# Turning activations into scan inputs: 32 transposes of 128x128 in place of 128 narrow ones

## The chip, the cores and the metric

The kernel runs on one core of one Trainium2 chip. The metric is the device time of one execution in microseconds, as the median of several runs. The profile is that of one further execution, whose span runs from its first to its last instruction.

## The reference, cut to what matters

Two blocks follow each other on a sequence of 256 rows of 2048 features. The first is a differential attention layer, a forgetting attention layer and their layer norms. The second is an S5 layer (a diagonal state space model), a gated output and an MLP. The change lies in the S5 layer, in how its inputs `u` are laid out:

```python
def s5_mixer(h_ctx, h_lat, ...):
    u_ctx, u_lat = to_groups(h_ctx), to_groups(h_lat)     # (1, 256, 128 groups, 16 features)
    for direction in range(2):
        ...
        st_ctx = s5_scan(uc_ctx, lam_bar, b_bar, s0, reverse)
        s_ctx_final = st_ctx[:, 0] if reverse else st_ctx[:, -1]
        st_lat = s5_scan(uc_lat, lam_bar, b_bar, s_ctx_final, reverse)
        y_lat = y_lat + jnp.einsum('btgp,ghp->btgh', st_lat, c_mat).real
```

`h_ctx` and `h_lat` are RMS-normed rows, scaled and shifted per feature: `h = modulate(rmsnorm(x), shift, scale)`. The context comes from the inputs alone; the latent rows are the output of the first block.

## The kernel before

The 256 rows are handled as 32 chunks of 8 rows. The scan works on a tile `U` (for the context) or `UL` (for the latent rows) with 128 partitions and 4096 columns: a partition is one of the 8 rows of a chunk (`q`) with one of the 16 features of a group (`h`), and the columns are 128 groups by 32 chunks. All of this happens twice: **run 0** is for the context, early, in the middle of the projection of the first layer; **run 1** is for the latent rows, after the last layer norm of the first block.

For each run the rows lie in `HC` with partition (a, c), where `a` (0 to 3) is a quarter of the features and `c` (0 to 31) the chunk, and with 8 by 512 columns. Within a quarter the 32 groups are split as e (0, 1) and j (0 to 15). The steps are:

1. `u_norm` works out the factor of each row. `turn` (VectorE for even q, ScalarE for odd q) multiplies the rows by it and writes them to `HT[run]` with columns ordered e, j, q, h. So for one (e, j) the 128 columns (q, h) are contiguous, and the partitions are (a, c).
2. `u_turn` (TensorE, line 2545) turns these blocks. There are 8 pieces. Piece pc takes a = pc // 2 and e = pc % 2, and does 16 transposes, each of the 32 partitions of one a by 128 columns. Each gives 128 partitions by 32 columns of a bank of PSUM, and 16 fill the bank's 512 columns. The instruction is a load of 32x128 weights and a matmul that streams 32 columns of the identity matrix. In the trace all of them carry line 2553.
3. `u_piece` (VectorE, line 1904) empties a bank in two operations on 128x512 elements: a multiplication by the scale of each group and feature (`FU[run]`, columns 0 to 127, one for each group, repeated over the 32 chunks) from PSUM to `U`, and, once that has ended, an addition of the shift (`FU[run]`, columns 128 to 255) in place. The helper `tt` at line 1424 records both, under the name `arena` in run 0 and `LT` in run 1.

The pieces use two banks of PSUM in turn (5 and 6), so that piece pc + 2 can be written once the first operation of piece pc has ended.

**Around run 0.** The projection streams its weights as 192 tiles of 128x512. ScalarE rounds a tile (line 972), VectorE subtracts for the rest (`tiles`, line 1424, `ring_lo`), TensorE does 6 matmuls for it (`pre_tile`, line 2279). The order is written out by hand: `U_AFTER = 180` puts one piece of `u_turn` behind each of the tiles 180 to 187, and VectorE runs two tiles ahead of the piece that it empties (`tiles(min(U_AFTER + pc + 2, ...))`, then `u_piece`). Behind the 192nd tile ScalarE copies the result, rounds the weights of the gate projection, and VectorE makes them ready; then come the 32 steps of `bl` (VectorE builds a 128x1024 matrix, TensorE turns it by 8 transposes of 128x128, line 2282; the matrices are stored as `m_state`; `v_chunk` multiplies them with `U`).

**Around run 1.** The layer norm ends, the rows are copied by DMA into `HC`, are scaled, and then TensorE does all 8 pieces in a row. Its next instruction, `v_chunk` for `("vl", f, i)`, waits for all of `u_made`. That stage is 1024 small matmuls (line 2279, `bank<-LT,ring`), in two halves f of 512; the scan of half f on VectorE (31 steps of four operations of 128x128 on `state(f, k)`, one after the other) needs the half's results, and the output matmuls of half f need the last step of its scan.

SyncE issues the loads of all weights in a fixed order to 6 slots (`ring`, line 701); each load waits until the slot's last reader is done.

Of the kernel before, what the change touches and what calls it, by code (L numbers as in the profile page):

```python
# [11 lines left out]
MUL, ADD, SUB, MAX, MIN = ALU.mult, ALU.add, ALU.subtract, ALU.max, ALU.min  # L12
# [269 lines left out]
def build(nc, A, out):  # L282
    ctx = ExitStack()
    with ctx:
# [18 lines left out]
        def filled(*key):  # L303
            i, n = bank_t.at[key]
            return FILLED[i], n

        def emptied(*key):
            i, n = bank_t.at[key]
            return EMPTIED[i], n

        def fill(*key):
            return FILLED[bank_t.at[key][0]], 1

        def bank(*key):
            return banks[bank_t.at[key][0]]
# [11 lines left out]
        ident = sb("ident", 128)  # L327
# [37 lines left out]
        def reg(off, n):  # L365
            return AR[:, off:off + n]
# [127 lines left out]
        def bl_at(b):  # L494
            return *bls[b % 2], bt
# [11 lines left out]
        HT = [reg(off, 4096).rearrange("p (e g q h) -> p e g q h", e=2, g=16, q=8) for off in (R3, 24576)]  # L507
        u_of, FU, FU_made = (U, UL), (reg(R5 + 3712, 256), LT[:, 4096:4352]), L1[:, 2048:2304]
# [33 lines left out]
        def a_p(i):  # L542
            return wk[i % 4].rearrange("p (c s) -> p c s", c=2)[:, :, 0:128 * (i % 2 + 1)]

        def a_stat(i):
            return stat[:, 8 * (i % 6):8 * (i % 6) + 8]
# [4 lines left out]
        def a_av(i):  # L551
            return aT_[:, i % 3 * 2:i % 3 * 2 + 2, :].rearrange("p a b -> p (a b)")
# [20 lines left out]
        def toep_at(i):  # L573

            return i // 4 + i % 4 // 2 * 2
# [844 lines left out]
        def vector_program(v):  # L1420
            o = Order(S)

            def tt(dst, x, y, op, *to):
                return v.tensor_tensor(dst, x, y, op).then_inc(*(to or o.up("dve")))  # L1424
# [16 lines left out]
            def empty(*key):  # L1441
                o.own = emptied(*key)
                return o.own[0], 1

            def own():
                v.wait_ge(*o.own)
# [451 lines left out]
            tiles(KK_AFTER[15] + 1)  # L1898
            corners(15)

            def by_group(run, i, n):
                return FU[run][:, i * 128:i * 128 + 128].unsqueeze(2).to_broadcast([128, 128, 32])[:, n, :]

            def u_piece(run, pc):

                gs = slice(16 * pc, 16 * pc + 16)
                v.wait_ge(*filled("u", run, pc))
                y = u_of[run][:, gs, :]
                tt(y, bank("u", run, pc)[:, :].rearrange("p (g c) -> p g c", g=16), by_group(run, 0, gs), MUL, *empty("u", run, pc))
                own()  # L1910
                tt(y, y, by_group(run, 1, gs), ADD, *o.up("u_made"))

            def u_norm(run):
                v.wait_ge(*filled("ss", run))
# [60 lines left out]
            for pc in range(8):  # L1975
                tiles(min(U_AFTER + pc + 2, 16 * N_PRE))
                u_piece(0, pc)
# [35 lines left out]
            for t in range(21):  # L2013
                if 0 <= t - 3 < 16:

                    i = t - 3
                    p, s_ = a_p(i), a_stat(i)
# [7 lines left out]
                if 0 <= t - 4 < 16:  # L2025
                    i = t - 4
# [9 lines left out]
                if 0 <= t - 1 < 16:  # L2036
                    i = t - 1
                    h, t2 = i // 2, i % 2
                    w_ = 128 * (t2 + 1)
                    p, s_ = a_p(i), a_stat(i)  # L2040
# [52 lines left out]
            for n in range(N_W1):  # L2093
# [35 lines left out]
                elif n == N_K + 5:  # L2129
# [3 lines left out]
                    for g3 in range(3):  # L2133
                        copy(lf3[:, :, 32 * g3:32 * g3 + 16], lf)
                        at = slice(32 * g3, 32 * g3 + 16)
# [33 lines left out]
            for pc in range(8):  # L2169
                u_piece(1, pc)  # L2170
# [106 lines left out]
        def tensor_program(p):  # L2277
            def mm(dst, l_, r_, start, stop):
                return p.matmul(dst, l_, r_, start=start, stop=stop, skip_group_check=True)  # L2279

            def tr(dst, src, k=128):
                return p.transpose(dst, src, ident[0:k, 0:k])  # L2282
# [3 lines left out]
            def room(*key):  # L2286

                i = bank_t.at[key][0]
                if i in said:
                    p.wait_ge(*emptied(*said[i]))  # L2290
                said[i] = key
# [212 lines left out]
            for j in range(8):  # L2504
# [4 lines left out]
                if j == 4:  # L2509
                    p.wait_ge(S["lam_cols"], 1)  # L2510
                    room("lam")
                    for i, s_ in enumerate((cr, ci, lbr, lbi)):
                        t = tr(bank("lam")[:, 128 * i:128 * i + 128], s_)
# [29 lines left out]
                t.then_inc(*fill("kk", ch))  # L2543

            def u_turn(run, pc):
                a_, e = pc // 2, pc % 2
                at = slice(32 * a_, 32 * a_ + 32)
                if pc == 0:
                    p.wait_ge(S["turn_v"], 4 * (run + 1))
                    p.wait_ge(S["turn_a"], 4 * (run + 1))  # L2550
                room("u", run, pc)
                for j in range(16):
                    t = p.transpose(bank("u", run, pc)[:, 32 * j:32 * j + 32], HT[run][at, e, j, :, :].rearrange("p q h -> p (q h)"),  # L2553
                                    ident[at, at])
                t.then_inc(*fill("u", run, pc))

            def u_sums(run):
# [22 lines left out]
            for pn in range(N_PRE):  # L2580
                for k in range(16):
                    pre_tile(16 * pn + k)
                    if pn == 1 and k < 8:
                        state(2 * k)
                        state(2 * k + 1)
                    for ch in range(16):
                        if KK_AFTER[ch] == 16 * pn + k + 1:
                            corners(ch)
                    done = 16 * pn + k + 1
                    if done == FU_AFTER:  # L2590
                        unit_factors()
                    if done == SS_AFTER:
                        u_sums(0)
                    if 0 <= done - U_AFTER < 8:
                        u_turn(0, done - U_AFTER)
                if pn in MOD_AT_PRE:
                    mod(MOD_AT_PRE[pn])
                if pn in SUMS_AT_PRE:
                    sums(SUMS_AT_PRE[pn])
# [13 lines left out]
            for b in range(33):  # L2613
                if b < 32:
                    p.wait_ge(S["blm"], b + 1)
                    for r in range(2):
                        room("bl", b, r)
                        for j in range(4):
                            t = tr(bank("bl", b, r)[:, 128 * j:128 * j + 128], bl_at(b)[r][:, 128 * j:128 * j + 128])
# [8 lines left out]
                if b in PART_AT_BL:  # L2628
                    j, q = PART_AT_BL[b]
# [6 lines left out]
            for t_ in range(21):  # L2636
                if 0 <= t_ - 5 < 16:
                    i = t_ - 5
                    h, t2 = i // 2, i % 2
# [4 lines left out]
                    for s in range(t2 + 1):  # L2644
                        t = mm(bank("ao", i)[:, 0:256], a_av(i)[:, 128 * s:128 * s + 128], vN[0][:, s, 256 * h:256 * h + 256],
                               s == 0, s == t2)
                    t.then_inc(*fill("ao", i))
                if 0 <= t_ - 4 < 16:
                    i = t_ - 4
                    p.wait_ge(S["amix"], i + 1)  # L2650
                    room("at", i)
                    for s in range(i % 2 + 1):
                        t = tr(bank("at", i)[:, 128 * s:128 * s + 128], wk[i % 4][:, 128 * s:128 * s + 128])
                    t.then_inc(*fill("at", i))
                if t_ < 16:
                    h, t2 = t_ // 2, t_ % 2
                    w_ = 128 * (t2 + 1)
                    room("as", t_)
                    for c in range(2):
                        t = mm(bank("as", t_)[:, 256 * c:256 * c + w_], qT[0][:, 2 * h + c, 128 * t2:128 * t2 + 128],  # L2660
                               kT[0][:, 2 * h + c, 0:w_], True, True)
                    t.then_inc(*fill("as", t_))
                if t_ in PART_AT_A:
                    j, q = PART_AT_A[t_]
# [6 lines left out]
            for n in range(N_W1):  # L2671
# [13 lines left out]
                if n == N_K + 6:  # L2685
                    room("nFT")
                    p.wait_ge(S["lf3"], 1)
                    for s in range(2):
                        t = mm(bank("nFT")[0:96, 0:256], lf3[:, s, :], tri[:, s, :], s == 0, s == 1)
                    t.then_inc(*fill("nFT"))  # L2690
                    room("FN")
                    for t2 in range(2):
                        for s in range(t2 + 1):
                            t = mm(bank("FN")[:, 16 * t2:16 * t2 + 16], tri[:, s, 128 * t2:128 * t2 + 128], lf[:, s, :], s == 0, s == t2)
# [9 lines left out]
            for pc in range(8):  # L2704
                u_turn(1, pc)
# [6 lines left out]
            for f in range(2):  # L2712
                p.wait_ge(S["step"], 31 * (f + 1))
                for i in range(4):
# [4 lines left out]
                    for i2 in (i, i + 4):  # L2719
                        cl[i2] = slot("cl", f, i2).rearrange("p (b d r x) -> p b d r x", b=2, d=4, r=2)  # L2720
                        e = toep_at(i2 - g4)
# [5 lines left out]
                    for j in range(4):  # L2727
# [7 lines left out]
                        for n, (i2, g2) in enumerate(four):  # L2735
                            t = mm(out_[n], UL[:, 32 * f + 4 * i2 + j + 64 * g2, :], wt[i2][:, 2 * (4 * g4 + j) + g2, :], False, True)
# [3 lines left out]
                for k in range(4 * f, 4 * f + 4):  # L2740
                    room("z", k)
                    for q in range(4):
                        t = tr(bank("z", k)[:, 128 * q:128 * q + 128], Y[:, k // 2, 4 * (k % 2) + q, :, :].rearrange("p g h -> p (g h)"))
# [63 lines left out]
```

## Time and profile before

| | |
|---|---|
| median of 3 runs | 2623.46 us (2622.78 to 2623.96) |
| span of the profiled execution | 2622.4 us |
| TensorE busy | 2418.2 us (92%) |
| VectorE busy | 1792.9 us (68%) |
| ScalarE busy | 1052.0 us (40%) |
| transposes of run 0 and run 1, line 2553 | 256, busy 22.0 us |

The time of the profiled execution by itself is not given, only its span; the median of the runs lies 1.1 us above that span. Busy time of TensorE counts each matmul until its result is out, so that overlapping ones make it look full; what a group of matmuls costs is read from the starts of its first instruction and of the first one behind it. `PEld` is the load of weights, which overlaps `PE`. A granted clock of 1.00 is 2.4 GHz and one of 0.50 is 1.2 GHz.

### The profile page before, as it was taken

What the parts mean: (1) busy time and instruction counts of PE and PEld (TensorE: products, weight loads), DVE (VectorE), ACT (ScalarE), POOL (GpSimd) and SP (SyncE); (2) the same over time, 40 slices, a digit from 0 to 9 for tenths busy, and PEclk for the clock granted to TensorE, in tenths of its full rate; (3) what the DMA queues carried; (4) which work ended last, traced back from release to release, by engine and by line L of the source; (5) the groups of instructions that cost most, each with busy time, mean ns of one, the idle gap of its engine ahead of it and who ended that gap; (6) DMA issues with size and microseconds to landing.
All of it is one profiled execution on the core that took longest, in us unless ns stands there. A gap on an engine that the chain in (4) does not pass through costs nothing.

```text
span 2622.4 us, 42441 instructions
## 1 busy us (share of the span) xinstructions
PE 2418.2 (92%) x17791; PEld 2018.3 (77%) x17791; DVE 1792.9 (68%) x2871; ACT 1052.0 (40%) x1588; POOL 183.4 (7%) x290
## 2 busy tenths in 40 slices
PE   5799999999889899989999696899799999999998
PEld 1488887777656698789887495688698998998986
DVE  4548887888767666877887648677654677655545
ACT  0243334454542323343662222444444443443443
POOL 1102433010100000112000000000000000000000
PEclk7699999999899899989999757999899999999999
DMA  9969999698877689979778897688455678655553
GB/s 352 338 233 345 364 363 323 205 344 321 302 292 274 225 305 327 379 267 316 241 256 312 230 338 298 221 283 278 140 181 189 225 272 281 216 184 189 190 166 108
DMA packets 317518, 699.75 MB, mean 267 GB/s; under 512 B 13648, under 2 KB 14160, under 8 KB 312464
## 3 DMA queue, kind: packets, MB, share of 16 engines
q1 hardware_dynamic: 298496, 627.29, 69.3%
q0 software_dynamic: 18560, 67.66, 7.2%
q8 instruction: 141, 2.31, 0.3%
q10 hardware_dynamic: 272, 2.10, 0.2%
q14 instruction: 49, 0.40, 0.0%
HBM read 646.78 MB, written 56.49 MB: 268 GB/s over the span
## 4 chain that ended last, share of the span: by engine, by line
PE 72%; DVE 13%; DMA 10%; ACT 2%; issue 1%; SPq 0%; DVEq 0%; POOL 0%; ACTq 0%
PE bank L2279 70%; DVE ring_lo L1424 3%; DMA ring<-in_w_mod 3%; DVE arena L1424 2%; DVE sm L1424 2%; DMA ring<-in_kv_w 2%; PE bank L2282 2%; DMA ring<-in_a_w_in 2%; DVE LT L1432 1%; DVE arena L1432 1%; DMA ring<-in_b_w_out 1%; PE bank L2553 1%; DMA m_state<-MSB 1%; DMA ring<-in_b_w_in 1%; ACT att_w_hi L1022 1%
## 5 line engine op out<-in xcount | busy, mean ns | idle before, releaser
L1424 DVE TENSOR_TENSOR ring_lo<-ring,w_hi 128x1024 fp32r<-128x1024 f32 (+1 forms) x380 | 428.2, 1134 | 355.0 <-ACT w_hi L1022 333.2
L1022 ACT CAST w_hi<-ring 128x1024 fp32r<-128x1024 f32 x316 | 330.2, 1048 | 471.8 <-PE bank L2279 471.7
L1022 ACT CAST att_w_hi<-ring 128x1024 fp32r<-128x1024 f32 x192 | 197.1, 1048 | 333.1 <-DMA ring<-in_kv_w 121.8
L1424 DVE TENSOR_TENSOR ring_lo<-ring,att_w_hi 128x1024 fp32r<-128x1024 f32 x192 | 233.8, 1221 | 132.0 <-ACT att_w_hi L1022 130.7
L2279 PE MATMUL bank<-in_hi,w_hi 128*128 128x256 f32 x1024 | 288.8, 282 | 1.1 <-ACT n L969 1.1
L2279 PE MATMUL bank<-in_lo,w_hi 128*128 128x256 f32 x1024 | 288.9, 282 | 0.0
L2279 PE MATMUL bank<-in_hi,ring_lo 128*128 128x256 f32 x1024 | 288.5, 282 | 0.0
L2279 PE MATMUL bank<-w_hi,hid_lo 128*128 128x512 f32 x640 | 254.2, 397 | 1.1 <-DVE ring_lo L1424 1.1
L2279 PE MATMUL bank<-att_w_hi,att_hi 128*128 128x512 f32 x512 | 211.6, 413 | 18.2 <-DVE ring_lo L1424 18.2
L2279 PE MATMUL bank<-ring_lo,att_hi 128*128 128x512 f32 x512 | 205.6, 402 | 0.0
L2279 PE MATMUL bank<-att_w_hi,att_lo 128*128 128x512 f32 x512 | 204.8, 400 | 0.0
L2279 PE MATMUL bank<-w_hi,hid_hi 128*128 128x512 f32 x512 | 202.6, 396 | 0.0
L972 ACT CAST in_lo<-ring 128x512 fp32r<-128x512 f32 x192 | 115.2, 622 | 215.2 <-PE bank L2279 117.7
L2279 PE MATMUL bank<-ring_lo,hid_hi 128*128 128x512 f32 x512 | 201.5, 394 | 0.0
L2279 PEld LDWEIGHTS bank<-in_hi,w_hi 128*128 128x128 f32 x1024 | 193.9, 189 | 1.4 <-ACT n L969 1.3
L2279 PEld LDWEIGHTS bank<-in_hi,ring_lo 128*128 128x128 f32 x1024 | 193.6, 189 | 0.0
L2279 PEld LDWEIGHTS bank<-in_lo,w_hi 128*128 128x128 f32 x1024 | 193.0, 188 | 0.1
L2279 PE MATMUL bank<-ring,cpad 128*32 128x512 f32 x1120 | 158.6, 674 | 22.6 <-DMA ring<-in_w_mod 18.3
L2279 PE MATMUL bank<-hid_lo,in_lo 128*128 128x256 f32 (+1 forms) x528 | 156.3, 296 | 15.6 <-DVE ring_lo L1424 15.2
L1424 DVE TENSOR_TENSOR ring_lo<-ring,in_lo 128x512 fp32r<-128x512 f32 x192 | 130.2, 700 | 55.8 <-ACT in_lo L972 55.7
L972 ACT COPY arena<-bank 128x512 f32<-128x512 f32 (+2 forms) x178 | 88.3, 582 | 172.7 <-PE bank L2279 154.7
L1432 DVE SCALAR_TENSOR_TENSOR LT<-ring,cpad,LT 128x512 f32<-128x512 f32 x195 | 146.7, 752 | 9.6
(278 smaller groups left out, 5106.1 us busy)
## 6 DMA issues: line engine op xcount, KB each, us to landing
ring<-in_w_mod SPq DMA_DIRECT2D x192, 1024.0 KB, 9.3
ring<-in_a_w_in SPq DMA_DIRECT2D x64, 1024.0 KB, 9.1
ring<-in_w_mlp_in SPq DMA_DIRECT2D x64, 1024.0 KB, 5.3
ring<-in_w_mlp_out SPq DMA_DIRECT2D x64, 1024.0 KB, 5.1
ring<-in_kv_w_mod SPq DMA_DIRECT2D x32, 1024.0 KB, 10.0
ring<-in_kv_w SPq DMA_DIRECT2D x32, 1024.0 KB, 7.9
ring<-in_b_w_in SPq DMA_DIRECT2D x32, 1024.0 KB, 5.7
ring<-in_s_w_glu SPq DMA_DIRECT2D x32, 1024.0 KB, 5.4
```

The source lines that it names most:

```text
L972: return a.copy(dst, src).then_inc(*(to or o.up("act")))
L1022: a.copy(whi(h), raw_half(h)).then_inc(*o.up("whi"))
L1424: return v.tensor_tensor(dst, x, y, op).then_inc(*(to or o.up("dve")))
L1432: return v.scalar_tensor_tensor(out=dst, in0=x, scalar=s1, in1=y, op0=o1, op1=o2).then_inc(*(to or o.up("dve")))
L2279: return p.matmul(dst, l_, r_, start=start, stop=stop, skip_group_check=True)
L2282: return p.transpose(dst, src, ident[0:k, 0:k])
L2553: t = p.transpose(bank("u", run, pc)[:, 32 * j:32 * j + 32], HT[run][at, e, j, :, :].rearrange("p q h -> p (q h)"), ident[at, at])
```

## The change

A piece now takes all four quarters a at once: pc gives e = pc // 4 and four values of j, and `u_turn` does 4 transposes of 128 partitions by 128 columns in place of 16 of 32 by 128. A bank then holds the columns (j, a, c). `u_piece` reads the bank in order, and the places in `U` and the factors in `FU` with strides: 4 values of j by 4 of a by 32 chunks, in runs of 32 columns, where before a piece was 512 contiguous columns of `U`. The number of elements, of pieces, of VectorE's operations, the banks and all waits are as before.

```diff
-            def by_group(run, i, n):
-                return FU[run][:, i * 128:i * 128 + 128].unsqueeze(2).to_broadcast([128, 128, 32])[:, n, :]
+            def by_group(run, i, e, j):
+                return (FU[run][:, i * 128:i * 128 + 128].rearrange("p (a e j) -> p e j a", a=4, e=2)[:, e, j]
+                        .unsqueeze(3).to_broadcast([128, 4, 4, 32]))
 
             def u_piece(run, pc):
 
-                gs = slice(16 * pc, 16 * pc + 16)
+                e, j = pc // 4, slice(pc % 4 * 4, pc % 4 * 4 + 4)
                 v.wait_ge(*filled("u", run, pc))
-                y = u_of[run][:, gs, :]
-                tt(y, bank("u", run, pc)[:, :].rearrange("p (g c) -> p g c", g=16), by_group(run, 0, gs), MUL, *empty("u", run, pc))
-                own()
-                tt(y, y, by_group(run, 1, gs), ADD, *o.up("u_made"))
+                y = u_of[run].rearrange("p (a e j) c -> p e j a c", a=4, e=2)[:, e, j]
+                tt(y, bank("u", run, pc)[:, :].rearrange("p (j a c) -> p j a c", j=4, a=4), by_group(run, 0, e, j), MUL,
+                   *empty("u", run, pc))
+                own()
+                tt(y, y, by_group(run, 1, e, j), ADD, *o.up("u_made"))
...
             def u_turn(run, pc):
-                a_, e = pc // 2, pc % 2
-                at = slice(32 * a_, 32 * a_ + 32)
+                e, j0 = pc // 4, pc % 4 * 4
                 if pc == 0:
                     p.wait_ge(S["turn_v"], 4 * (run + 1))
                     p.wait_ge(S["turn_a"], 4 * (run + 1))
                 room("u", run, pc)
-                for j in range(16):
-                    t = p.transpose(bank("u", run, pc)[:, 32 * j:32 * j + 32], HT[run][at, e, j, :, :].rearrange("p q h -> p (q h)"),
-                                    ident[at, at])
+                for j in range(4):
+                    t = tr(bank("u", run, pc)[:, 128 * j:128 * j + 128], HT[run][:, e, j0 + j, :, :].rearrange("p q h -> p (q h)"))
                 t.then_inc(*fill("u", run, pc))
```

## Rows read from the trace of the kernel before

**Rows 1.** Head of the page: span, TensorE's busy time.
```profile
span 2622.4 us, 42441 instructions
PE 2418.2 (92%) x17791; PEld 2018.3 (77%) x17791; DVE 1792.9 (68%) x2871; ACT 1052.0 (40%) x1588; POOL 183.4 (7%) x290
```

**Rows 2.** Timeline, run 0, one period: start us, length us, engine, operation, idle before.
```profile
467.00 1.07 PEld L2553 LDWEIGHTS bank<-ident,arena 32*128 32x128 f32 x16 [0.36 <-issue]
...
468.11 0.19 PEld L2279 LDWEIGHTS bank<-in_lo,hid_lo 128*128 128x128 f32 x1
...
468.22 0.69 DVE L1424 TENSOR_TENSOR arena<-bank,arena 128x512 f32<-128x512 f32 x1 [0.67 <-PE bank L2553]
...
468.94 0.69 DVE L1424 TENSOR_TENSOR arena<-arena 128x512 f32<-128x512 f32 x1
...
469.55 0.69 DVE L1424 TENSOR_TENSOR ring_lo<-ring,in_lo 128x512 fp32r<-128x512 f32 x1
469.70 1.07 PEld L2553 LDWEIGHTS bank<-ident,arena 32*128 32x128 f32 x16 [0.36 <-issue]
```

**Rows 3.** Chain that ended last, end of run 0: start us, length us, what.
```profile
484.33 7.20 PE bank L2279 x30
...
492.04 0.63 ACT w_hi L972
```

**Rows 4.** Windows, run 0: us, busy of PE, PEclk, DMA share, GB/s.
```profile
470.00:475.00 5.00, 5.00 (x43) 1.00 0.02 5
```

**Rows 5.** Timeline: transposes of 128x128 at clock 1.00 and at 0.50.
```profile
505.65 0.85 PEld L2282 LDWEIGHTS bank<-ident,arena 128*128 128x128 f32 x8 [0.84 <-issue]
506.47 0.19 PEld L2279 LDWEIGHTS bank<-w_hi,hid_lo 128*128 128x128 f32 x1
...
1124.35 3.67 PE L2282 MATMUL bank<-ident,arena 128*128 128x128 f32 x16 [6.27 <-DVE arena L1429]
1125.50 1.02 ACT L969 ACTIVATE arena<-bank,MODC,st 128x256 f32<-128x256 f32 x2 [1.18 <-PE bank L2282]
```

**Rows 6.** Timeline: VectorE and TensorE behind run 0.
```profile
490.02 1.29 DVE L1424 TENSOR_TENSOR arena<-arena 128x512 f32<-128x512 f32 x2
...
491.37 0.86 PEld L2282 LDWEIGHTS bank<-ident,arena 128*128 128x128 f32 x8 [0.29 <-DVE arena L1424]
...
492.69 1.90 DVE L1424 TENSOR_TENSOR ring_lo<-ring,w_hi 128x512 fp32r<-128x512 f32 x3 [1.38 <-ACT w_hi L972]
```

**Rows 7.** Timeline, run 1: the turns and VectorE's pieces.
```profile
1509.78 12.52 PEld L2553 LDWEIGHTS bank<-ident,arena 32*128 32x128 f32 x128 [11.64 <-issue]
...
1511.73 0.69 DVE L1424 TENSOR_TENSOR LT<-bank,LT 128x512 f32<-128x512 f32 x1 [3.12 <-PE bank L2553]
...
1513.44 0.69 DVE L1424 TENSOR_TENSOR LT<-bank,LT 128x512 f32<-128x512 f32 x1 [0.29 <-PE bank L2553]
1514.16 0.69 DVE L1424 TENSOR_TENSOR LT<-LT 128x512 f32<-128x512 f32 x1
1514.77 0.68 DVE L1424 TENSOR_TENSOR LT<-bank,LT 128x512 f32<-128x512 f32 x1
...
1523.95 36.27 PE L2279 MATMUL bank<-LT,ring 128*64 128x32 f32 x676 [1.51 <-DVE LT L1424]
```

**Rows 8.** Windows, run 1 and the stage behind: us, busy of PE, PEclk, DMA share, GB/s.
```profile
1509.70:1522.50 12.80, 12.63 (x128) 0.50 1.02 426
...
1524.00:1560.00 36.00, 36.00 (x676) 0.50 0.91 315
```

**Rows 9.** Chain that ended last, from run 1 on.
```profile
1523.95 27.55 PE bank L2279 x512
...
1625.35 15.76 PE bank L2279 x379
```

**Rows 10.** Timeline: a VectorE operation that reads `state(f, k)` in four runs of 32.
```profile
1553.26 0.29 DVE L1424 TENSOR_TENSOR sm<-arena,LS 128x128 f32<-128x128 f32 x1
```

**Rows 11.** Chain that ended last, in the second layer.
```profile
1038.37 11.46 DMA ring<-in_kv_w
```

**Rows 12.** SyncE's waits over the span: us in total, times, longest us.
```profile
SPq L701 <- PE bank L2279: 1706.2, 396, 24.9
```

**Rows 13.** Timeline: 32 matmuls of the same form as behind run 1, at clock 1.00.
```profile
510.86 1.12 PE L2279 MATMUL bank<-arena,MSB 128*64 128x32 f32 x32
```

## The prediction

> **What bounds the kernel now.** I read the page first. TensorE is busy for 92% of the span [rows 1]; that says that it is usually the engine to look at, not that every microsecond taken from it counts. The change touches two short places, so I read each by its timeline and then by the chain of work that ended last, to see who waits for whom.
>
> In run 0 the turns lie between the tiles of the projection. One period goes from the first weight load of one piece to that of the next: 467.00 to 469.70, so 2.70 us [rows 2]. Of it the 16 narrow transposes take 467.00 to 468.11, 1.11 us; the tile and the gap behind it take the remaining 1.59. VectorE has three operations in a period and then sits idle for 0.67 us until TensorE has filled the next bank. It starts at 468.22, 468.94 and 469.55, and the third lasts 0.69: 2.02 us of work. So TensorE sets the pace in run 0. Its clock is 1.00 there, and the DMA engines are nearly idle (share 0.02) [rows 4], so weights aren't what the tiles wait for. The chain agrees: behind the last piece it stays on TensorE until the last tile at 491.5, then goes over ScalarE's rounding at 492.04 [rows 3].
>
> In run 1 all 128 transposes follow each other at clock 0.50 and take from 1509.78 until the last bank is full; the small matmuls start at 1523.95 [rows 7], so the whole step takes 14.17 us. TensorE is busy for 12.63 of 12.80 us [rows 8]. VectorE is late by the first piece (it starts 1.95 us after TensorE) and then waits again at every second piece: 0.29 us ahead of 1513.44, none ahead of 1514.77, and so on. The step lies on the chain, which goes on over the first 512 small matmuls, VectorE's scans and the output matmuls from 1625.35 [rows 9].
>
> **The change, run 0.** It takes out 16 transposes a piece and puts in 4 of 128x128. Their price is on hand: in the `bl` stage 8 of them go from 505.65 to the next weight load at 506.47, 0.82 us, at the same clock [rows 5]. That is 0.103 each, so 0.41 for 4. For the ones that end a burst I add a little and take 0.45; from above, PEld's 0.86 for 8 and a tail [rows 6] could make it 0.55. A piece gets shorter by 1.11 - 0.45 = 0.66 us (bounds 0.56 and 0.70), and the period falls to 2.04. The gap of 0.36 ahead of the transposes I leave as it is.
>
> Can VectorE follow? It needs 2.02 us in a period and some 0.05 to react to a filled bank, 2.07 against 2.04. It may fall behind by 0.03 a piece, 0.3 us over 8, but TensorE doesn't feel that: VectorE is two tiles ahead, and a bank comes free after the first of three operations. Over 8 pieces TensorE wins 8 x 0.66 = 5.3 us. What is late next? VectorE's own work behind run 0 ends at 490.02 + 1.29 = 491.31 and TensorE's transposes for it begin at 491.37; VectorE then idles 1.38 us until ScalarE has rounded weights, which waits for TensorE's last tile [rows 6]. So VectorE can lose up to 1.38 us there before it is the later one, and it loses 0.3. I take 5.3 us, with bounds 8 x 0.56 = 4.5 and 8 x 0.70 = 5.6.
>
> A rule can be laid beside this row. The Trainium skill (TensorE: Matmul & The Clock Gate, LDWEIGHTS) says that a weight load takes its columns divided by 1.2 GHz, whatever the rows, so that a 32x128 load costs as much as a 128x128 one. That is an estimate of 107 ns for both, 1.71 us for 16, and a gain of 1.28 us a piece, or 10.3 us in run 0. The trace agrees with it for the wide ones (103 ns) and not for the narrow ones, which take 69 ns each [rows 2]; the measurement decides, and nothing in my sum comes from the rule.
>
> **The change, run 1.** At clock 0.50 a burst of 16 transposes of 128x128 lasts 3.67 us, and the reader of the first four starts 1.15 us after the burst did [rows 5]. So a piece costs TensorE some 0.9 us and a bank is readable 1.15 after the piece's start. VectorE needs 1514.77 - 1513.44 = 1.33 us for the two operations of a piece [rows 7]. Now VectorE is the slower one: it starts at 1509.78 + 1.15 = 1510.93 and goes through 8 pieces without a wait, 7 x 1.33 + 1.42 = 10.73, to 1521.66. Do the two banks hold this? Piece pc + 2 may start 0.69 after VectorE began pc and is readable 1.15 later, at 1.84, before VectorE wants it at 2.66. The small matmuls start 0.06 behind, at 1521.7 in place of 1523.95: 2.2 us. The bound below is that of a piece that costs VectorE 0.1 more in strides, 1.4; above, an immediate first bank, 2.5.
>
> **Strides on VectorE.** I cost them at nothing. The scan's first product reads a state as four runs of 32 columns with strides, 128 elements, in 0.29 us [rows 10]; a contiguous 512 takes 0.69 [rows 7], which is 0.40 for 384 more elements, 1.04 ns each. 128 elements at that rate leave 0.16 fixed for either kind, so runs of 32 show no surcharge. That row has its strides on one input; here output, input and factors have them, which no row shows. The lower bound is zero, since the number of elements stays; the upper one is in the rivals.
>
> **Behind the two places.** For the gains to reach the end nothing may be tied to a fixed time. Loads are issued when a slot comes free, and SyncE spends 1706 us waiting for TensorE to free one [rows 12], so an earlier TensorE makes earlier loads. In run 1 the six loads in flight run at 426 GB/s; the stage behind eats them at 315 [rows 8], so starting it 2.2 us earlier doesn't starve it.
>
> The sum: 5.3 + 2.2 = 7.5 us off a span of 2622.4, so 2614.9; the runs' median stands 1.1 above the span, so 2616.0. Within this case I expect 2614.5 to 2618.
>
> **Rivals.**
>
> *Half of it is swallowed.* The chain crosses loads again and again in the second layer, one of 11.46 us at 1038.37 [rows 11]. Where such a load is late because the DMA engines are full and not because its slot came late, it lands at its old time and run 0's gain stops there. Then only run 1's 2.2 us and perhaps a part of the 5.3 remain: 2621.3 with none of it, 2618.6 with half. For it: the many such entries. Against: the idle DMA in run 0 [rows 4] and SyncE's waits for slots. Chance 0.27.
>
> *The clock rises in run 1.* If the wide transposes, which stream 128 columns in place of 32, bring the clock to 1.00, the stage behind starts at that level. 32 matmuls of its form at clock 1.00 take 1.12 us with a tail of 0.2 [rows 13], 0.03 each, so 512 would take 15 in place of 27.55 us, and the whole would come to 2616.0 - 12.5 = 2603.5. Against it: TensorE was busy all through 12.8 us of transposes and 36 us of small matmuls, and the clock stayed at 0.50 [rows 8]. The Trainium skill (TensorE: Matmul & The Clock Gate, Part 4) says that a transpose doesn't count as busy for the clock; by that, nothing changes here, and this trace agrees as far as the narrow ones go. Chance 0.06.
>
> *Slower.* VectorE pays for strides. If they double each of its operations, 0.69 to 1.38, a piece costs it 1.33 + 1.38 = 2.71 us in run 1, 21.7 for 8, against the 12.2 from 1511.73 to 1523.95 now; with a start 0.8 earlier that is 8.7 us lost. In run 0 its period becomes 2.02 + 1.38 = 3.40 against 2.70, 5.6 us lost. Together 14.3: 2637.8. It decides from about 0.35 us an operation on, where run 0 is level with 2.70 (2.02 + 2 x 0.35 = 2.72) and run 1 has lost 3.2. Rows 10 speak against it. Chance 0.07.
>
> **How the numbers follow.** The main case has 0.60. The prediction is its 2616.0 us, 0.28% faster. A measurement of this kernel tells about 0.2% from no change, here 5.2 us, so the line is at 2618.2. Faster: 0.54 of the main case's 0.60 (its slow edge crosses the line), 0.06 for the clock, 0.03 of the swallowed case: 0.63. Same: 0.06 + 0.24 = 0.30. Slower: 0.07. The range for 8 in 10 leaves out the clock, the slow rival and the end of the swallowed case: 2611 to 2622.
>
> **What would show it.** In run 0: 4 transposes a piece in 0.41 to 0.45 us, a period near 2.05, VectorE's wait gone from 0.67 to under 0.1, the last tile ending at 486.2. In run 1: VectorE without waits behind its first piece, operations still at 0.69, the small matmuls starting 11.9 us after the first transpose and not 14.2, clock still 0.50. Behind both: every later stage shifted by 5.3 and then 7.5 us. The prediction is wrong if VectorE's operations are longer than 0.69, if the wide transposes take longer between tiles than in `bl`, or if the shift shrinks at a load in the second layer.

## The result

The changed kernel took 2606.75 us as the median of 5 runs (2604.06 to 2612.34), the kernel before 2622.78 beside it (2621.16 to 2623.96). The ratio is 0.9943 (95% interval 0.9929 to 0.9957): 15 us less, with 11 to 19 as the interval. The forecast was 7.5 us less and a range down to 2611, so the sign was right and the size wrong by a factor of two. Two more sets of the same kernel, of 6 and 5 runs on two chips, gave 0.9946 (0.9931 to 0.9961) and 0.9954 (0.9941 to 0.9966): 14 and 12 us.

The profile of the changed kernel comes from the slowest of its five runs (2612.34 us, span 2610.6), so it shows 11.8 us less than [rows 1] and not 15. Line numbers have moved by two: tiles and small matmuls are line 2281, all transposes of 128x128 line 2284.

**Run 0.** First the chain that ended last, then the timeline of one piece (start us, length us, what; the numbers answer to [rows 2]).

```profile
464.91 0.44 PE bank L2284 x4
465.35 1.39 PE bank L2281 x6
466.73 0.44 PE bank L2284 x4
...
485.91 0.63 ACT w_hi L972
```

```profile
466.11 0.19 PEld L2281 LDWEIGHTS bank<-in_lo,in_hi 128*128 128x128 f32 x1
466.34 0.59 PEld L2284 LDWEIGHTS bank<-ident,arena 128*128 128x128 f32 x4
466.57 0.60 PE L2284 MATMUL bank<-ident,arena 128*128 128x128 f32 x4
466.72 0.69 DVE L1424 TENSOR_TENSOR ring_lo<-ring,in_lo 128x512 fp32r<-128x512 f32 x1
...
466.90 0.19 PEld L2281 LDWEIGHTS bank<-in_lo,hid_lo 128*128 128x128 f32 x1
...
467.32 0.69 DVE L1424 TENSOR_TENSOR arena<-bank,arena 128x512 f32<-128x512 f32 x1
```

A period is now 0.44 + 1.39 = 1.83 us, where it was 2.70 and the forecast 2.04. By the chain, which goes by ends, the four transposes cost 0.44, and the tile takes 1.39 and not 1.59. By the starts of weight loads, as the prediction counted, the burst costs 0.56 (466.34 to 466.90), just over the upper edge of 0.55 that it had set, and the rest of the period 1.27. Either way the piece is 0.87 us shorter, and what shrank beside the burst is the tile's share: the weight load of the first wide transpose starts 0.23 us after the tile's last one (466.34 after 466.11), at the tile's own pace, and the 0.36 us of idle time that stood ahead of each narrow burst is gone. VectorE's operations still last 0.69 us. It starts a piece every 1.93 us and falls slightly behind TensorE, without effect, as expected. The rounding at 492.04 [rows 3] is at 485.91.

**Run 1.** The timeline, to be laid beside [rows 7].

```profile
1499.18 1.57 PEld L2284 LDWEIGHTS bank<-ident,arena 128*128 128x128 f32 x8 [8.66 <-issue]
...
1500.34 0.69 DVE L1424 TENSOR_TENSOR LT<-bank,LT 128x512 f32<-128x512 f32 x1 [2.33 <-PE bank L2284]
...
1501.68 0.69 DVE L1424 TENSOR_TENSOR LT<-bank,LT 128x512 f32<-128x512 f32 x1
...
1511.10 1.04 PEld L2281 LDWEIGHTS bank<-LT,ring 128*64 128x64 f32 x18 [2.66 <-DVE LT L1424]
```

VectorE starts 1.16 us after TensorE, takes 1.33 to 1.34 us a piece without a wait, and the small matmuls start 11.92 us after the first load, against 14.17 before. The forecast was 11.9. This place gives 2.25 us.

To see where the rest is, I took VectorE's instructions, which are the same 3250 in the same order in both kernels, and subtracted start from start. Between the tiles of run 0 and the stage behind it the difference grows by 6.66 us, in run 1 by 2.25: 8.9 together. The other 3 us of this profile, and 3 to 6 of what the three sets of runs show, come from stretches that the change doesn't touch. The experiments are mostly about these.

### The profile page after: what moved, and what is told of

It is laid out like the page before. It is cut to its first block, busy times and chain, and to the rows that moved or that the text cites. A ratio compares the mean times of both kernels' runs of the same rounds, so it can differ in the third digit from the quotient of the medians.

```text
span 2610.6 us, 42057 instructions
## 1 busy us (share of the span) xinstructions
PE 2410.5 (92%) x17599; PEld 2008.8 (77%) x17599; DVE 1792.1 (69%) x2871; ACT 1051.9 (40%) x1588; POOL 186.1 (7%) x290
## 3 DMA queue, kind: packets, MB, share of 16 engines
q8 instruction: 139, 2.28, 0.4%
## 4 chain that ended last, share of the span: by engine, by line
PE 70%; DVE 16%; DMA 10%; ACT 2%; issue 1%; SPq 1%; DVEq 0%; ACTq 0%
PE bank L2281 68%; DVE ring_lo L1424 4%; DVE arena L1424 3%; DMA ring<-in_w_mod 3%; DVE sm L1424 2%; DMA ring<-in_a_w_in 2%; PE bank L2284 2%; DVE LT L1432 2%; DMA ring<-in_kv_w 2%; DVE arena L1432 2%; DMA ring<-in_b_w_out 1%; DVE MSB L1424 1%; DMA ring<-in_b_w_in 1%; DMA ring<-in_kv_w_mod 1%; DMA arena<-arena 1%
## 5 line engine op out<-in xcount | busy, mean ns | idle before, releaser
L2281 PE MATMUL bank<-att_hi,att_w_hi 128*128 128x256 f32 x512 | 148.7, 291 | 5.5 <-issue 2.3
```

## The experiments

All times are against the kernel before, run beside them on the same chip, by the ratio of the runs.

**1. Each part alone, and both kernels once more.** The first is the kernel before without an edit, the fourth the changed one. In the second and third the new forms are used for one run only:

```diff
+                if run in STRIDED:          # (0,) or (1,)
+                    ...wide transposes / strided places, as in the change
+                    return
```

> The kernel before, once more, for a second profile and as a measure of what is chance. Measured so far: 16 us less for the change, where I had forecast 7.5. In the two profiles the stretch of run 0 is 6.7 us shorter and that of run 1 is 2.2 us shorter; the rest lies between and behind (4 to 7 us). Theory A (the rest is earned: later stages gain from the shift): this profile's milestones stand within 1 us of the first profile of before everywhere. Theory B (the rest is chance in one profile): milestones at 700 to 740, 1430 to 1510 and 1800 to 1900 us move by 2 to 4 us between two executions of the same kernel. Time within 2 us of 2623.

> Wide transposes and strided pieces for run 0 alone. If the two gains add up with nothing behind them: -6.7 us. Theory A1 (the extra comes from run 0's shift, which lets stages up to 1500 us start earlier against their loads): -11 to -14 us. Theory A2 (the extra comes from run 1's place, with the layer norm and the stages behind): -6.7 us. If strides cost VectorE anything, run 0's first operation of a piece is over 0.69 us.

> Wide transposes and strided pieces for run 1 alone. Additive: -2.2 us. Theory A1: -2.2 us, and all milestones ahead of 1509 us as before. Theory A2: -5 to -9 us, with the extra between 1524 us and the end.

> The changed kernel once more, for a second profile: its first was that of the slowest of five executions (2612.3 of 2604 to 2612). Time 2604 to 2609. If that profile's late loss of 3.5 us between 1800 and 1900 us was chance, this one doesn't have it, and the shift against before stays near -15.5 us from 1700 us to the end.

The kernel before came out at 0.9998 (0.9989 to 1.0007). Run 0 alone gave 0.9957 (0.9942 to 0.9971), 11.3 us less. Run 1 alone gave 0.9985 (0.9973 to 0.9996), 3.9 us less. The local gains are the same in every profile of these forms: 6.6 to 6.8 us for run 0 and 2.25 for run 1. So each part gives more than its place shows, run 0 4.6 us (1 to 8.5 by the interval) and run 1 1.7 us (the interval allows none), between its two forecasts. Single profiles of one kernel, the first and the second of before, differ by 1 to 4 us in several stretches, so chance is part of it. For run 0 the interval leaves at least 1 us beyond it.

**2. Moving the code blocks.** TensorE's instructions come in by DMA. The page of the changed kernel has a queue for them, with 139 packets in place of 141:

```profile
q8 instruction: 139, 2.28, 0.4%
```

2.28 MB in 139 packets are 16.4 KB each, for some 36,000 instructions in all, so about 256 instructions a packet. The chain has stops at that distance. In the kernel before, in the output matmuls:

```profile
1641.11 0.53 issue
1641.64 4.80 PE bank L2279 x127
1646.44 1.51 issue
1647.95 4.95 PE bank L2279 x128
1652.90 1.27 issue
```

From 1641 us on TensorE stands still every 128 matmuls, each with its load, so every 256 instructions, for 0.5 to 1.5 us and for nothing that the profile shows as a wait; the 379 matmuls ahead of that pass without a stop. The trace's DMA records tie the stops to the code: packets of the queue above end at 1640.14, 1646.44 and 1652.75, and TensorE goes on 1.50, 1.51 and 1.41 us behind them. From the end of run 1 to the end of the stretch B below, the 17 profiles have 52 stops of 1 us and more that are put down to "issue"; 46 of them end 1.2 to 1.6 us behind the end of such a packet, while the packets there are some 6.4 us apart. The change takes 96 transposes out of each run, 192 instructions, and so moves all later boundaries in the program's text. Padding does the same without the change:

```diff
+            for _ in range(32):          # 64, 96, 128, 192
+                p.transpose(banks[4][0:32, 0:32], ident[0:32, 0:32], ident[0:32, 0:32])
             p.wait_ge(S["rows"], 16 * len(row_copies))
```

TensorE waits until 13.9 us there anyway; the longest padding ends at 12.0 us in its trace.

> The kernel before with 32 small transposes (64 instructions) of the identity put ahead of TensorE's first work, where it waits for the first rows. TensorE's instructions are fetched by DMA in blocks of 16 KB, 256 instructions each (141 packets of 16 KB for its 36,000 instructions before, 139 with the change). The change takes 192 instructions out in each run, so behind run 0 every block boundary falls 192 instructions later in the program's text (the same as 64 earlier); 64 more instructions at the start give the same alignment without the change. Theory F (what was gained beyond the local 8.9 us comes from where the blocks' boundaries fall): 3 to 5 us less than before, the wait for the load at 1438 us down from 9.8 to 7.4 us. Theory C (it is the shift in time, or chance): within 1.5 us of before.

> The same with 64 small transposes (128 instructions): the alignment that the full change gives behind run 1, without the change. Theory F: 3 to 6 us less than before, with less idle time put down to issue in the output matmuls of 1625 to 1655 us. Theory C: within 1.5 us of before.

> The changed kernel with 96 small transposes (192 instructions) at the start: between run 0 and run 1 the blocks' boundaries fall as in the kernel before. Theory F: 2 to 4 us more than the changed kernel, so about 10 to 12 under before, the wait for the load near 1431 us back at 9 to 10 us. Theory C: as the changed kernel, 14 us under before.

> The changed kernel with 192 small transposes (384 instructions) at the start: behind run 1 the boundaries fall as in the kernel before. Theory F: the gains beyond the local ones are gone, 9 us under before. Theory C: 14 us under before. If the small transposes last longer than TensorE's first wait, the early stage shows it as a delay ahead of 120 us, and it is to be taken off.

Measured: 0.9995 (0.9986 to 1.0005), 0.9989 (0.9978 to 0.9999), 0.996 (0.9948 to 0.9973) and 0.997 (0.9958 to 0.9982), so 1.3, 2.9, 10.5 and 7.9 us less. The gains of the padded kernel before are smaller than the boundaries theory said (the first is within the 1.5 us of the other theory; by the plain medians of the runs they are 3.0 and 5.2). The padded changed kernel came out about where it said, though not beside the unpadded one. Then a padding of one whole block, which moves no boundary:

> The kernel before with 128 small transposes at the start: 256 instructions, one whole block of code, so the boundaries fall where they did. So far 32 of them gave 1.3 us less and 64 gave 2.9 less by the ratio of the runs, and the wait for the load at 1438 us is 8.3 to 9.9 us in the four profiles whose boundaries lie there as in before, and 7.1 to 7.5 in the six others. Theory F (boundaries): as before within 1.5 us, the load's wait 8.3 us or more. Theory P (the padding itself helps, by what it does to the first microseconds): 3 us or more under before, the load's wait by chance.

> The changed kernel with the same one block of padding. Theory F: as the changed kernel, 14 us under before (192 small transposes gave only 8). Theory P: another 2 to 6 us away from the changed kernel.

0.9993 (0.9982 to 1.0003) and 0.9935 (0.9921 to 0.9949): 1.8 and 17 us less. A whole block leaves both kernels where they were within their intervals. The load's wait was 8.19 us in the first, just short of the 8.3 I had put down. The span of its one profile is 2611.7 us, against 2622.4 and 2621.1 for the two of the kernel before with the same boundaries, so the total of a single profile decides nothing here.

Last, the pair on one chip, and run 0's gain with every later boundary as in the kernel before:

> The changed kernel on the same chip as its padded version: 14 to 16 us under before.

> The changed kernel with 192 small transposes at the start, once more. Theory F (boundaries of the code's blocks): again some 6 us above the changed kernel beside it, about 8 us under before. Theory C (the first difference of 6 us was between chips and by chance): within 2 us of the changed kernel beside it.

> The change in run 0 alone, with 96 small transposes at the start: from the end of run 0 to the end of the kernel every block boundary falls exactly as in the kernel before. Theory F: only the local gain of 6.7 us is left, where the version without padding gave 11.3, and the wait for the load near 1432 us is 8.2 us or more. Theory C: 11 us under before, the load's wait at 7.1 to 7.5.

0.9954 (0.9941 to 0.9966), 0.9958 (0.9943 to 0.9972) and 0.9968 (0.9955 to 0.9981): 12.1, 11.0 and 8.4 us less. The pair differs by 1 us and not by 6, which taken alone speaks for chance; 8.4 lies between 6.7 and 11.3; and the load's wait was 7.97 us in the last, again just short of what the theory of the boundaries wants (8.2). The intervals are 3 to 4 us to either side, so by total times this batch doesn't decide. All sets of the changed kernel together lean the other way: 15, 14, 12 and 17 us less with the boundaries at their own places (the last a whole block off), and 10.5, 7.9 and 11.0 with paddings that move them.

The traces decide better than the totals, since they can be cut. Two stretches hold the difference (of each, one wait was named before the paddings ran; the bounds were not): **A**, the second layer's end, from VectorE's start at 1380.0 us of the kernel before to its start at 1480.2 (behind run 0, ahead of run 1); **B**, the output matmuls and what follows, from 1625.0 to 1682.3 (behind run 1). For every profile I took the length of the stretch and by how many instructions, less whole blocks of 256, the boundaries had moved there (192 fewer instructions count as 64):

| boundaries moved by | A, us | B, us |
|---|---|---|
| 0 | 100.2, 97.5, 97.6, 98.5, 96.3, 97.2 | 57.3, 56.9, 56.5, 57.0, 56.4, 55.7, 58.6 |
| 64 | 94.2, 95.6, 94.1, 94.6, 94.4, 95.2 | 55.9, 54.0, 54.7, 54.5 |
| 128 | 95.5, 94.5, 93.8 | 54.5, 52.7, 53.7, 52.7, 52.3 |
| 192 | 96.9, 97.3 | 53.8 |

The rows mix kernels with and without the change. Row 0 of A has the kernel before, run 1 alone, the change with 96 paddings and run 0 alone with 96; row 64 has run 0 alone, the kernel before with 32 paddings and the changed kernel four times. Row 0 of B has the changed kernel with 192 paddings twice and the version with transposes of 64 partitions. No length of row 0 overlaps one of row 64 or 128, in either stretch but for one of 55.9 against 55.7. So it isn't the change itself and not the shift in time: run 0 alone with 96 paddings has run 0's shift and is in row 0 (96.3 and 57.0), and the kernel before, without any of the change, has 95.2 in A with 32 paddings and 52.3 in B with 64. The changed kernel's boundaries moved by 64 in A and by 128 in B. The mean of row 0 against that of the changed kernel's four own profiles is 97.9 - 94.6 = 3.3 us in A and 56.9 - 53.4 = 3.5 us in B.

In A 1.4 us of it, in the mean, are one load. In the chain of the kernel before and of the changed one:

```profile
1438.45 9.80 DMA ring<-in_b_w_out
```

```profile
1431.20 7.36 DMA ring<-in_b_w_out
```

It is 8.0 to 9.9 us in the six profiles of row 0, and 6.9 to 7.6 in the nine of rows 64 and 128 (the two of row 192 have 7.45 and 8.41). The load itself is slower; no packet of code moves while it is under way, in either of these two profiles. In B the stops are fewer and elsewhere. The chain of the second profile of the changed kernel:

```profile
1612.33 21.60 PE bank L2281 x569
1633.93 0.61 issue
1634.54 2.63 PE bank L2281 x70
1637.17 0.86 issue
```

1.5 us of stops, against 4.2 in the kernel before with the 0.84 at its end. Over all of B, TensorE's stops of 0.3 us and more that are put down to "issue" add up to 4.2 to 4.8 us in the seven profiles of row 0 (mean 4.4) and to 1.8 to 3.0 (mean 2.2) in the four of the changed kernel, so they account for 2.2 of the 3.5 us. They don't account for every profile: run 1 alone has 4.3 us of them and is at 54.0.

**3. The gap ahead of the narrow transposes.** Transposes of 64 partitions, 8 a piece, in both runs, with strides on VectorE as in the change (shortened, and set against the changed kernel):

```diff
-                for j in range(4):
-                    t = tr(bank("u", run, pc)[:, 128 * j:128 * j + 128], HT[run][:, e, j0 + j, :, :]...)
+                rows = slice(pc // 2 % 2 * 64, pc // 2 % 2 * 64 + 64)      # j0 = pc % 2 * 8
+                for j in range(8):
+                    t = p.transpose(bank("u", run, pc)[:, 64 * j:64 * j + 64], HT[run][rows, e, j0 + j, :, :]..., ident[rows, rows])
```

> Transposes of 64 partitions by 128 columns, 8 a piece, for both runs, with the same strides on VectorE. In run 0 the gap of 0.36 us ahead of the narrow transposes is gone with the wide ones: their weights are loaded while the last matmul of the tile still runs. Theory G (a load for part of the rows waits for the full-array matmuls ahead of it): the gap stays at 0.3 to 0.4 us with 64 rows, the 8 transposes take 0.5 to 0.9 us, the period is 2.3 to 2.5 us. Theory H (it is the number of instructions in the burst): the gap is about halved, and the period near 2.25.

0.9966 (0.9954 to 0.9977). The timeline of run 0:

```profile
465.77 0.40 PE L2298 MATMUL bank<-in_lo,in_hi 128*128 128x512 f32 x1
...
466.10 0.57 PEld L2575 LDWEIGHTS bank<-ident,arena 64*128 64x128 f32 x8 [0.37 <-issue]
...
466.73 0.19 PEld L2298 LDWEIGHTS bank<-in_lo,hid_lo 128*128 128x128 f32 x1
```

The gap is whole, 0.37 us, with 8 transposes in place of 16 and 64 rows in place of 32. The period is 2.22 us (466.10 to 468.32 in the trace), under both forecasts. It isn't the count of the burst, and the next experiment, with 8 transposes of all 128 rows, has no gap: its first load starts 0.23 us behind the last one of the tile. The gap comes with a load for a part of the array's rows behind matmuls of all rows. The Trainium skill (TensorE: Matmul & The Clock Gate, Part 3) says that a weight load overlaps a running matmul only when their row groups differ, though it also has loads to the background buffer pulled ahead. These rows don't bear the first out as it stands: the load that has all the rows of the matmul ahead of it goes ahead without a gap, the ones that have a quarter or a half of them don't. A shortened load also costs less: 0.63 for 8 is 79 ns with 64 rows, beside 69 with 32 and 103 to 110 with 128.

**4. Who sets the pace of run 0.** Each wide transpose of run 0 twice:

```diff
-                for j in range(4):
+                for j in (0, 1, 2, 3, 0, 1, 2, 3) if run == 0 else range(4):
```

> The changed kernel with each wide transpose of run 0 issued twice, 8 a piece. If TensorE sets the pace there, a piece gets 4 x 0.11 = 0.44 us longer, the period 1.83 + 0.44 = 2.27 and the end of run 0 3.5 us later. If VectorE set it (its three operations need 2.02 us), the period would go from 2.02 to 2.27 and the end would move by less than 2 us.

```profile
466.40 0.87 PE bank L2284 x8
467.28 1.39 PE bank L2281 x6
468.67 0.87 PE bank L2284 x8
```

The period is 2.27 us, as TensorE's sum says. Run 0's local gain falls from 6.66 to 3.41, by 3.25 us of the 3.5. The time was 0.9969 (0.9955 to 0.9982).

## Why the prediction was wrong in size

- *16 transposes out, 4 in, for 0.45 us*: near. The chain has 0.44 for 4; by the starts of weight loads, the prediction's own measure, they cost 0.56, 0.11 more than forecast and just over its upper edge of 0.55.
- *"The gap of 0.36 ahead of the transposes I leave as it is"*: wrong, and it cost the first part of the error. The gap belonged to the narrow load and went with it: the time from the tile's last load to the burst fell from 0.55 to 0.23 us. With the 0.11 above against it a piece won 0.87 us and not 0.66, run 0 6.7 us and not 5.3. [Rows 5] would not have said so: their wide burst has 0.84 us of idle time ahead of it, behind matmuls with 32 columns of weights. But other rows of the same trace, at clock 1.00, have wide transposes behind matmuls with 128x128 weights, as in run 0, and no idle time:

```profile
696.38 0.30 PEld L2279 LDWEIGHTS bank<-arena,MSB 128*128 128x128 f32 x2 [1.08 <-issue]
696.41 0.67 PE L2279 MATMUL bank<-arena,MSB 128*128 128x256 f32 x2 [0.92 <-issue]
696.70 0.35 PEld L2282 LDWEIGHTS bank<-ident,LT 128*128 128x128 f32 x2
```

- *VectorE can follow, and has 1.38 us to lose*: right in effect. It needs 1.93 us a piece, less than the 2.02 that I had added up, and is now the slower one by 0.10 us; nothing waits for it.
- *Run 1*: right, 11.92 us against 11.9 forecast, 2.25 against 2.2.
- *Strides at nothing*: right, but not by its working. The rate of 1.04 ns an element was drawn from one strided and one contiguous operation, and so the fixed 0.16 us comes out the same for both whatever strides cost. The runs show it: all strided operations take 0.68 to 0.69 us, with strides on output, input and factors. The rival "slower" is out.
- *The clock rises in run 1*: it didn't. TensorE ran 32 wide transposes over 10.3 us at clock 0.50 and went on at 0.50:

```profile
1499.20:1509.50 10.30, 8.57 (x32) 5.85 (x32) 8.91 (x14) 0.00 (x0) 0.00 (x0) 0.50 1.01 425
```

- *Half of it is swallowed by loads*: not half. Between run 0 and A the shift came and went by 1 to 4 us, as between two profiles of before, and was back in the mean. Ahead of run 1 some of it was: the copy of the rows takes 15.27, 13.49, 15.20 and 13.81 us in the chains of the four profiles of the changed kernel (the last padded by a whole block), and 13.4 to 13.6 in the five of the kernel before, 0.9 us more in the mean.
- *The sum, "5.3 + 2.2 = 7.5 us", with "every later stage shifted by 5.3 and then 7.5 us"*: this is the step that failed most. It asks only what could be lost behind the two places and has no term for what 384 fewer instructions do there, so it puts that at nothing without a reason. The profiles show 3.3 us in A and 3.5 in B, where the boundaries of TensorE's code blocks fall elsewhere.

The account: 6.66 + 2.25 + 3.3 + 3.5 = 15.7 us. Against it stand the 0.9 us of the copy and a loss behind the gated output, from 1801 to 1901 us: that stretch takes 99.5 to 99.8 us in the five profiles of the kernel before, padded or not, but 103.2, 99.7, 99.7 and 103.4 in the four of the changed kernel. In the long ones the clock rises and falls back once more behind TensorE's pause (windows of PE alone: us, busy, PEclk, DMA share, GB/s; first the changed kernel's first profile, then its second):

```profile
1859.80:1864.80 5.00, 2.21 (x13) 0.82 0.00 0
1864.80:1869.80 5.00, 5.00 (x25) 0.50 0.02 5
```

```profile
1857.40:1862.40 5.00, 2.99 (x23) 1.00 0.01 3
1862.40:1867.40 5.00, 5.00 (x44) 1.00 0.01 2
```

With 1.8 us for that as the mean of four, the account comes to 13.0. The spans of the same four profiles lie 13.7 us in the mean under those of the three of the kernel before in row 0, and the four sets of runs gave 15, 14, 12 and 17.

What is shown: the two local gains (in all profiles), that with full-height loads the gap goes away, that the length of A and B goes with where the boundaries fall and not with the change, and in B that TensorE's stops follow the landing of code. What is only argued: that the fetch of a block has to do with the load of A, beside which none was under way. What stays open: the size of it in total time. The changed kernel with 192 paddings was 6 us short of the unpadded one measured on another chip, and 1 us short of it side by side; and the kernel before gained 1.3 and 2.9 us from padding, where the row means of A and B let one expect some 5 and 7. So of the 3 to 8 us that the sets of runs have beyond the local 8.9, these stretches explain a part that the totals don't fix. The second fall of the clock is in none of the five profiles of the kernel before and in eight of the twelve with some of the change, three of them with the boundaries of that stretch where the kernel before has them (twice 192 paddings, and the transposes of 64 partitions). So it isn't the boundaries there; its cause wasn't tried.

## What to carry to other kernels

When narrow operations on TensorE stand between full ones, read the idle time ahead of the burst as part of their price: here it was 0.36 us beside 1.11. A change in the number of instructions moves every later code block, which in the profiles here went with some 3 us in each of two stretches, beside 6.7 and 2.25 for the change itself; measure such a change with padding beside it before believing the last microseconds. And compare stretches of several traces, with the same engine's instructions matched one to one: that separated 2.25 us cleanly in kernels whose totals are uncertain by 3.

## What the runs showed of the hardware

A load of weights of 32, 64 and 128 rows by 128 columns takes 69, 79 and 103 to 110 ns in a burst of transposes at clock 1.00. Behind matmuls on all rows with 128x128 weights, one of 32 or 64 rows first waits 0.36 to 0.37 us, and one of 128 rows doesn't; behind matmuls with 128x32 weights a load of 128x128 stands 0.84 us behind the last load's end [rows 5]. TensorE's code comes in packets of 16.4 KB, about 256 instructions, and in a stage of small matmuls a boundary can cost 0.5 to 1.5 us (1641 to 1654 us of the kernel before), or nothing (the 379 matmuls ahead of it); TensorE goes on 1.2 to 1.6 us behind a packet's end in 46 of 52 stops of 1 us and more. Strided runs of 32 columns on output and both inputs cost VectorE nothing in a 128x512 operation (0.68 to 0.69 us, as contiguous). Of small matmuls, 1012 in a window of 54 us back to back behind run 1 ran at a granted clock of 0.50 throughout, with the DMA engines 93% busy.
